# Two transformer blocks on one core: norm factors from sums formed during the output projection, and the next layer's first projection in pairs of tiles

## What is computed

```python
def rms_norm_2(x, g):
    return x * lax.rsqrt(jnp.mean(x * x, axis=-1, keepdims=True) + EPS) * g

def mixer_layer(x, ctx, ...):
    hx = rms_norm_2(x, g_pre) * (1.0 + scale_x) + shift_x
    hc = rms_norm_2(ctx, g_pre) * (1.0 + scale_c) + shift_c
    ... = in_proj(hx, w_in), in_proj(hc, w_in)      # first of it: the latent q (384 columns)
    ...                                             # three branches, attention
    out_x = merge_branches(...) @ w_o
    x = x + gate_x * rms_norm_2(out_x, g_post)
    if update_ctx:                                  # only in the first of the two layers
        ctx = ctx + gate_c * rms_norm_2(out_c, g_post)
```

## Time and profile before

| | us |
|---|---|
| median of three runs (lowest, highest) | 2761.8 (2761.8, 2762.77) |
| the profiled execution | 2760.01 |
| its span in the trace | 2758.2 |
| PE busy in it | 2548.8 (92%) |
| DVE / ACT / POOL busy | 1156.1 / 874.9 / 532.6 |

### The profile page before, as it was taken

How to read it: one execution, slowest core, us unless ns; L and a number is a source line. 1 busy time by engine, 2 the same in 40 slices (tenths; PEclk the granted TensorE clock), 3 DMA queues, 4 the chain that set the end, 5 groups by cost and what they waited for, 6 DMA issues and landing times.

```text
span 2758.2 us, 33891 instructions
## 1 busy us (share of the span) xinstructions
PE 2548.8 (92%) x13851; PEld 1979.4 (72%) x13851; DVE 1156.1 (42%) x1907; ACT 874.9 (32%) x1589; POOL 532.6 (19%) x398
## 2 busy tenths in 40 slices
PE   7888889899999898999989999999698999899998
PEld 5655667677788675578866888888465577678876
DVE  3645544553444426442266223223435533642433
ACT  3325542432222214432145211212324432532222
POOL 3004212321111212220022110122313210221023
PEclk8997999999999899999999999999789999999998
DMA  4231151344422210102200122122110123013232
GB/s 157 78 93 31 47 168 61 108 153 153 153 92 91 87 30 20 39 24 62 84 9 16 46 84 62 46 77 100 48 30 21 39 69 107 1 47 114 77 92 92
DMA packets 188636, 200.59 MB, mean 73 GB/s; under 512 B 15640, under 2 KB 183288, under 8 KB 187970
## 3 DMA queue, kind: packets, MB, share of 16 engines
q1 hardware_dynamic: 184866, 178.23, 21.0%
q10 hardware_dynamic: 3616, 20.19, 1.9%
HBM read 187.92 MB, written 10.49 MB: 72 GB/s over the span
## 4 chain that ended last, share of the span: by engine, by line
PE 82%; DVE 7%; ACT 5%; POOL 3%; issue 3%; DMA 1%; ACTq 0%; POOLq 0%; SPq 0%; DVEq 0%
PE PS L682 20%; PE PS L683 20%; PE PS L685 20%; PE PS L764 5%; PE PS L791 4%; PE PS L777 2%; PE PS L1110 2%; DVE ST L1778 1%; ACT SA L1266 1%; PE PS L726 1%; DVE WL L1710 1%; POOL RB L2412 1%; PE PS L833 1%; PE PS L889 1%; PE PS L860 1%
## 5 line engine op out<-in xcount | busy, mean ns | idle before, releaser
L682 PE MATMUL PS<-HH,WH 128*128 128x512 f32 x2144 | 797.0, 372 | 36.7 <-POOL HL L2417 19.6
L683 PE MATMUL PS<-HL,WH 128*128 128x512 f32 x2144 | 764.6, 369 | 0.0
L685 PE MATMUL PS<-HH,WL 128*128 128x512 f32 x2144 | 692.4, 367 | 0.0
L1710 DVE TENSOR_TENSOR WL<-WB,WH 128x2048 fp32r<-128x2048 f32 (+2 forms) x150 | 313.2, 2088 | 640.6 <-ACT WH L1199 632.7
L682 PEld LDWEIGHTS PS<-HH,WH 128*128 128x128 f32 x2144 | 405.4, 189 | 155.4 <-issue 29.7
L683 PEld LDWEIGHTS PS<-HL,WH 128*128 128x128 f32 x2144 | 405.9, 189 | 73.9 <-issue 1.9
L685 PEld LDWEIGHTS PS<-HH,WL 128*128 128x128 f32 x2144 | 366.7, 189 | 46.6
L1199 ACT ACTIVATE WH<-WB 128x2048 fp32r<-128x2048 f32 (+2 forms) x150 | 256.3, 1708 | 362.3 <-PE PS L685 290.5
L2437 POOL TENSOR_SCALAR SA<-SA,ST 128x768 f32<-128x768 f32 (+3 forms) x80 | 141.1, 1764 | 451.8 <-DVE ST L1792 451.8
L2412 POOL TENSOR_TENSOR RB<-RB,SA 128x512 f32<-128x512 f32 (+2 forms) x68 | 92.7, 1363 | 429.6 <-ACT SA L1216 428.0
L1266 ACT ACTIVATE SA<-PS,ST 128x768 f32<-128x768 f32 (+3 forms) x160 | 118.8, 743 | 94.7 <-DVE ST L1778 94.3
(11 more groups left out here) (324 smaller groups left out, 3420.5 us busy)
## 6 DMA issues: line engine op xcount, KB each, us to landing
WB<-in_w_in_dram SPq DMA_DIRECT2D x67, 1024.0 KB, 5.3
WB<-in_w_ff_dram SPq DMA_DIRECT2D x32, 1024.0 KB, 5.5
WB<-in_w_mod_dram SPq DMA_DIRECT2D x24, 1024.0 KB, 5.3
WB<-in_w_branch_dram SPq DMA_DIRECT2D x24, 512.0 KB, 3.5
WB<-in_w_o_dram SPq DMA_DIRECT2D x8, 1024.0 KB, 5.6
XTc<-xd ACTq DMA_DIRECT2D x2, 3072.0 KB, 10.1
WB<-in_cmp_w_dram SPq DMA_DIRECT2D x4, 1024.0 KB, 5.5
WB<-in_w_mkv_dram SPq DMA_DIRECT2D x4, 1024.0 KB, 5.2
```

Of the source, the lines that this page charges most:

```text
L682: pe.matmul(D[0:m, d + o:d + o + w], h, xh[:, o:o + w], start=first, stop=False)
L683: pe.matmul(D[0:m, d + o:d + o + w], h, xl[:, o:o + w], start=False, stop=False)
L685: t = pe.matmul(D[0:m, d + o:d + o + w], lo, xh[:, o:o + w], start=False, stop=last)
L1710: dve.tensor_tensor(WL[s % NH][:, 0:b.kt, 0:b.cols], WB[b.n % NW][:, 0:b.kt, 0:b.cols], WH[s % NH][:, 0:b.kt, 0:b.cols].bitcast(F32), ALU. ...
```

## The change

It has four parts.

1. **o0 and the two norms.** ACT alone empties the PSUM tiles of `o0`: it squares straight from PSUM (scale 0.5), copies to `OT` already multiplied by gate and gain (`GM`, to which the 0.5 has moved), and for layer 0 also squares that copy ("oo") and the residual's tiles ("xx"). DVE forms the products of residual and `OT` ("cross") and their sum in `AC1`, and the sum of "xx" in `AC0`; POOL adds "oo" in `AC2` beside the squares of `o0`. The next norm's sum is then xx + 2·r·cross + r²·oo, with r the first norm's factor. PE sums seven sets of columns, DVE combines them on 6 columns (`uv`), ACT roots, and both factors are spread. The wide sums, the wide root and the wide inverse go.
2. **The loop over layer 1's tiles.** Scaling `OT` (DVE, now without the gain), the residual addition (POOL) and the tiles' norm go through one loop, tile by tile. In both layers the shift of even tiles moves from DVE to ACT (in place, then the copy to `HH`). The spill goes in four DMAs, the last after tile 7. The weights of `ql`'s second block are split inside the loop.
3. **`ql` in a pair.** `linear_pair` computes output tiles 0 and 1 together: per input tile both tiles' matmuls. Layer 0's ctx factor is made ahead of the x factor.
4. **Sums without the last addition, tables ahead.** For `h0x` and `o1`, PE sums the accumulated seven squares and the eighth apart (`sum_columns_late`), so POOL's last addition goes. Activations of one column (`TL`) load ACT's table for Exp before the attention and for Sqrt before `o{l}`.

```diff
+            def linear_pair(name, x, n, freed, ready):
+                b = of[name][0]
+                Ds = [slot((name, j), *freed(j)) for j in range(2)]
+                wh, wl = whole(b)
+                for k in range(b.kt):
+                    for r in ready(k):
+                        pe.wait_ge(*at(*r))
...
+                    for j, D in enumerate(Ds):
...
+            def sum_columns_late(N, nf, n, *freed):
+                D = slot(("norm", N), *freed)
+                pe.wait_ge(*at("nadd", N, nf - 2))
+                add_columns(D, 0, n, RB[rb[N]], True, False)
+                pe.wait_ge(*at("sq", N, nf - 1))
+                add_columns(D, 0, n, SA[sa[N, nf - 1]], False, True).then_inc(*done("nsum", N))
...
+                    D = slot(("norm", N), ("on", l, 7))
+                    pe.wait_ge(*at("nadd", N, 6))
+                    add_columns(D, 0, nt, RB[rb[N]], True, False)
+                    E = slot(("norm", "h1"), ("hn", "h1x", 7), ("hn", "h1c", 7))
+                    pe.wait_ge(*at("xadd", 7))
+                    add_columns(E, 0, nt, AC[0], True, False)
+                    pe.wait_ge(*at("nadd", "oo", 6))
+                    add_columns(E, 6, nt, AC[2], False, False)
+                    pe.wait_ge(*at("sq", N, 7))
+                    add_columns(D, 0, nt, SA[sa[N, 7]], False, True).then_inc(*done("nsum", N))
+                    pe.wait_ge(*at("cross", 6, "sum"))
...
+                    spread_columns(N, nt)
+                    spread_columns("h1", nt)
```

ACT, layer 1's loop and the end of the layer:

```diff
+                        shift = MOD[:, l, f, s_:s_ + 1]
+                        if f % 2 == 0:
+                            act.wait_ge(*at("hm", N, f))
+                            D = SD[sd["hn", N, f]][:, 0:n]
+                            act.activation(D, D, ACT.Identity, bias=shift).then_inc(*done("hb", N, f))
+                            act.wait_ge(*at("hb", N, f))
+                            act.activation(HH[:, f, o:o + n], D, ACT.Copy).then_inc(*done("hh", N, f))
...
+                    if l == 1 and f % 2:
+                        act.wait_ge(*at("xt_p", 0, f))
+                        act.dma_start(XD[:, f - 1:f + 1, :], XTc[:, f - 1:f + 1, :]).then_inc(...)
                 act.wait_ge(*at("spill", l + 1))
...
+                act.activation(TL[:, :], EP[:, :], ACT.Sqrt)
...
+                    act.activation(D[:, 0:nt], P(N, j)[:, 0:nt], ACT.Square, scale=0.5).then_inc(*done("sq", N, j))
+                    for o, n, s_ in segs[l]:
+                        t = act.activation(OT[:, j, o:o + n], P(N, j)[:, o:o + n], ACT.Copy, scale=GM[:, l, 1, j, s_:s_ + 1])
```

DVE and POOL:

```diff
+                        for f in {3: (0, 1), 4: (2, 3), 5: (4,), 6: (5, 6), 7: (7,)}.get(j, ()):
+                            cross(f)
+                        for f in {3: (1,), 4: (2, 3), 5: (4, 5), 6: (6, 7)}.get(j, ()):
+                            residual(f)
...
+                    dve.wait_ge(*at("nbc", "o0"))
+                    out_part(0)
+                    inverse("h1", 6)
+                    out_part(1)
+                    dve.wait_ge(*at("nbc", "h1"))
                 for f in range(8):
+                    if l and 0 < f < 7:
+                        out_part(f + 1)
+                    if f == 3:
+                        begin(f"ql{l}")
+                    dve.wait_ge(*at(*(("xt_p", 0, f) if l else ("xf", 3, 7))))
...
+                for f in range(8):
+                    if l == 1:
+                        residual(0, f, NT)
+                    if f % 2 == 0:
                         for N, o, n in ((f"h{l}x", 0, NX), (f"h{l}c", NX, NC)):
                             low_half(N, f, HL[:, f, o:o + n], HH[:, f, o:o + n])
```

More of the change, by code:

```diff
@@ L422, in build @@
             ot = sb("ot", 128, 4, 1024, scope=s2)
+            AC, QS = [sb(f"AC{i}", 128, NT, scope=s2) for i in range(3)], sb("QS", 128, 8, scope=s2)
         rows, _ = vec_layout()
@@ L688, in linear @@
                             after(j)
+            def linear_pair(name, x, n, freed, ready):
[5 more added lines that the diff above has]
+                        pe.wait_ge(*at(*r))
+                    xh, xl = x(k)
+                    for j, D in enumerate(Ds):
+                        h, lo = (w[:, k, 128 * j:128 * j + 128] for w in (wh, wl))
+                        for o, w in cols_of(n):
+                            pe.matmul(D[:, o:o + w], h, xh[:, o:o + w], start=k == 0, stop=False)
+                            pe.matmul(D[:, o:o + w], h, xl[:, o:o + w], start=False, stop=False)
+                        for o, w in cols_of(n):
+                            t = pe.matmul(D[:, o:o + w], lo, xh[:, o:o + w], start=False, stop=k == b.kt - 1)
+                        if k == b.kt - 1:
+                            t.then_inc(*done("lin", name, j))
             def linear_tok(b, x, ready, ntok, *freed, pace=0):
@@ L720, in sum_columns, with add_columns @@
                 t.then_inc(*done("nsum", N))
+            def add_columns(D, c0, n, src, first, last):
+                for c in range(n // 128):
+                    t = pe.matmul(D[:, c0 + c:c0 + c + 1], src[:, c * 128:(c + 1) * 128], cm("ones")[:, 0:1],
+                                  start=first and c == 0, stop=last,
+                                  skip_group_check=True)
+                return t
+            def sum_columns_late(N, nf, n, *freed):
[4 more added lines that the diff above has]
+                add_columns(D, 0, n, SA[sa[N, nf - 1]], False, True).then_inc(*done("nsum", N))
             def spread_columns(N, n):
@@ L1162, in tensor_program @@
                 merge(2)
[L1164 removed]
+                drain(linear(f"o{l}", hx(nt), nt, lambda j: [("ot_a", l, j)],
                              lambda k: [("ml_d" if k % 2 else "ml_p", l, k)]))
[L1166 to L1172 removed]
+                N = f"o{l}"
+                if l == 1:
+                    sum_columns_late(N, 8, nt, ("on", l, 7))
+                    spread_columns(N, nt)
+                else:
+                    D = slot(("norm", N), ("on", l, 7))
[9 more added lines that the diff above has]
+                    pe.wait_ge(*at("cross", 6, "sum"))
+                    add_columns(E, 12, nt, AC[1], False, False)
+                    pe.wait_ge(*at("cross", 7))
+                    add_columns(E, 12, nt, SD[sd["cross", 7]], False, True)
+                    pe.wait_ge(*at("sq", "oo", 7))
+                    add_columns(E, 6, nt, SA[sa["oo", 7]], False, True).then_inc(*done("nsum", "h1"))
+                    spread_columns(N, nt)
+                    spread_columns("h1", nt)
             for h in range(2):
@@ L1212, in sq @@
                     D = taken(rb, RB, N, freed)
+                elif f == last:
+                    D = taken(sa, SA, (N, f), freed)
                 else:
-                    D = taken(sa, SA, (N, f), ("nadd" if freed is not None else "nacc", N, f))
+                    D = taken(sa, SA, (N, f), ("nadd", N, f))
                 act.wait_ge(*at(*ready))
@@ L1598, in scalar_program @@
                 root(f"kvn{l}", NT, 256)
+                act.activation(TL[:, :], EP[:, :], ACT.Exp)
                 for half in range(2):
@@ L2380, in vector_program, with cross, residual @@
                 m_low(7)
+                N = f"o{l}"
+                def cross(f):
+                    D = AC[1] if f == 0 else taken(("cross", f), ("nsum", "h1") if f == 7 else ("cross", f, "sum"))
+                    dve.wait_ge(*at("ot_a", l, f))
+                    dve.tensor_tensor(D[:, 0:nt], XTc[:, f, 0:nt], OT[:, f, 0:nt], ALU.mult).then_inc(*done("cross", f))
+                    if 0 < f < 7:
+                        dve.wait_ge(*at("cross", f))
+                        dve.tensor_tensor(AC[1][:, 0:nt], AC[1][:, 0:nt], D[:, 0:nt], ALU.add).then_inc(*done("cross", f, "sum"))
+                def residual(f):
+                    dve.wait_ge(*at("sq", "xx", f))
+                    if f > 1:
+                        dve.wait_ge(*at("xadd", f - 1))
+                    dve.tensor_tensor(AC[0][:, 0:nt], AC[0][:, 0:nt], SA[sa["xx", f]][:, 0:nt], ALU.add).then_inc(*done("xadd", f))
                 for j in range(8):
```

168 lines of the change are left out of this document (87 added, 81 removed).

## The result

The changed kernel takes 2735.1 us as the median of four runs (2733.8 to 2738.4), beside 2762.3 for the kernel before on the same chip (2761.8 to 2762.8): the ratio is 0.9899, 95% interval 0.9885 to 0.9912. It is 27.2 us faster. Forecast were 2750 and a range of 2740 to 2758: the sign was right, the size less than half of what came.

A forecast was written before the change was run, and what follows sets the result against it. TensorE was taken as the bound nearly everywhere, so only stretches where it waits could pay. Terms 7.8 - 2 + 3.6 + 2.5 = 11.9 us off 2760.0 gave 2748.1, as a median 2750, range 2740 to 2758.

The forecast's parts named there:

- B: Between the layers, o0's end to kvl1: DVE starts 11.2 us earlier, but longer loop rounds leave kvl1 2 us later.
- D: Table loads: Exp's 1.28 us load before each layer's first attention unit moves to where ACT idles, 2.5 us less.
- A: Layer 0's entry: computing the first two ql output tiles as a pair ends 7.8 us earlier; bounds 9.5 and 0.
- worst case: Whole kernel, without the slow-DVE rival: the terms' low ends, 5 - 6 + 2.8 + 2, gain only 3.8 us, 2758.
- C: End of the kernel: POOL's last addition and the table load go, 3.6 us less (2.8 to 4.2).
- the page's sum: Table loads at 1.38 us more draining each, by the skill page: C and D some 4 us better, time 2746.
- The Sqrt load ... nothing: In front of o0 and o1: the load delays a weight split needed 8 us later, so costs nothing.
- 1, the loop overlaps: Layer 1's tile loop: POOL never kept waiting, so 14 us gained instead of 2 lost, 2734; chance 12%.
- 2, DVE late beside o0: Beside o0: 21 DVE operations at 2.2 us each end late and delay TensorE's sums, 6 us slower, 2768; chance 6%.
- 3, the clock stays low in the pair: Layer 0's ql pair: TensorE's clock stays low, so A gains nothing, 2758; chance 12%.
- 4, all sums at the full clock: Sums between the layers: all passes run at full clock, so B gains 5 us instead, 2743; chance 12%.

The follow-up runs named there:

- the base: The changed kernel run once more with nothing edited, as reference for the follow-ups: 2734.1 us, ratio 0.9904 to the kernel before.
- TL alone: The kernel before with the four-byte-wide tile TL only allocated, no instruction added, moving everything allocated behind it by 32 bytes: 2757.8 us, ratio 0.9988.
- early-factor order: Changed kernel, but o0's norm factor summed and spread first, so DVE's scalings and POOL's additions run beside the remaining sums: 2717.4 us, ratio 0.9838.

## Why the forecast was right and wrong, point by point

The result lies below the range. Three things failed: the balance at the end of B, the size of D, and a term for the addresses that the sum did not have.

**A, right.** 8.5 us where 7.8 stood: DVE's start stayed (7.4 us behind the feed-forward stage against 7.7), the pair ran without a gap. With single tiles 6.9 of it went, so most of A is the pair. The forecast had nothing for what follows: the sums over `ql` and `kvl` ran in part at the low level in every trace with layer 0's pair (0.72 over them in the base, 1.00 in the kernel before), and 1.3 to 3.4 us went back. They did so too without a pair in the traces with TL alone (65.2), with Sqrt's load besides (65.3) and with the pad ahead of `HH` on the kernel before (65.7); so the pair is not needed for it. What sets where the clock falls was not tested. The forecast's worst case counts A at 5 us, though its own bound for A was 0; the result lies at the other end.

**B, the chain right, the balance wrong.** Sums to 15.9 us behind `o0` (forecast 15.8), DVE's start 22.9 (23.1), rounds of 9.1 to 10.1 us (9.4), POOL idle 3.6 us in each (3 to 4). The step that failed is the chain of spill and weights to "`kvl1`", at "2022.3. **2 us more** than before". The spill's last quarter was issued 58.3 us behind `o0` (forecast 61.1) and done 3.3 us after that, not 4.3; the weights' low half was ready (2006.6) before the third tile's matmuls were through. So `kvl1` started right behind them, 68.6 us behind `o0`, where the forecast had 71.9 and the kernel before 69.9. With 1.3 gained instead of 2 lost the term is off by 3.3. The second traces give 2.2 up to `kvl1`'s copy.

**C, right.** 4.3 on average where 3.6 stood (2.8 to 4.2), 3.5 between the first two traces; the sums took 1.9 us where 2.1 stood. From the last sum to the scaling the forecast's times left 2.2 us, and it took 2.6 to 2.7 in both kernels, without the load.

**D, mis-sized.** "2.5 us less" was the load's own length, twice. In its place it measured 5.1, and the run without it lost 8.6. The missing part in its place is the granted clock, which had fallen behind the wait in these traces; in the one with TL alone it had not in layer 0, and there the load cost its length only. The forecast had cited the Trainium skill ("ScalarE: Activation LUTs", What ACT_TABLE_LOAD costs), which puts 1.38 us of draining on each load. The trace has the activation 0.02 us behind the load, and TensorE's wait grew by 1.28 us, so no such drain shows. By the page's sum the forecast would have been nearer, for another reason. "The Sqrt load ... nothing" was true of the delay that it meant: no matmul of `o0` waited. But the load left a chain between the layers too, worth 2.3 by one pair of traces, which the forecast had inside B without a price.

**A term was missing.** Nothing in the forecast concerned the allocation of TL. It is 3 to 6 us, visible only as 395 against 391 ns in matmuls that the change does not touch.

**The rivals.** *1, the loop overlaps*: not in this kernel. Its counter-argument, that the low half stands in POOL's queue behind the addition, was the right one, and changing just that order gave 8 us. *2, DVE late beside o0*: the 21 operations took 0.94 to 2.6 us, 1.42 on average (forecast 1.3, harmless up to 1.4), and let TensorE wait only 0.38 us. *3, the clock stays low in the pair*: no, 0.88 over it. *4, all sums at the full clock*: no, the first 12 passes took 1.40 us, the next 24 took 4.11, then it was 2.70 for 12. In the early-factor order the passes took 0.12 to 0.13 us each until 11 us behind o0's end, and only the last set 2.70 for 12; there TensorE has the spread's 128-column matmuls between them.

Of the 15 us between forecast and result, an estimate from these differences gives 3 to 6 to addresses, 3 to 6 to D and 3 to 4 to B, less 2 to 3 given back behind A. What remains is within the spread between executions: the kernel before ran from 2756.8 to 2767.1 over all its runs.

## What to carry to other kernels

Price a stall on a chain by its length and by what TensorE's matmuls behind it take at the level to which the clock has fallen; here 1.28 us cost 1.3 where the clock stayed high and 2.5 to 4.1 where it fell. Where two norms follow each other, finish what depends on the first factor while the second one's sums are still being made, and never put an operation directly behind one on which it depends through other engines if an independent one is at hand. Before believing a difference of a fifth of a per cent, compare runs that were made beside each other, compare the durations of untouched instructions, and see whether an allocation moved; where TensorE is the bound, try the addresses of data against weights.

## What the runs showed of the hardware

- A 512-column matmul on split fp32 (low half of the data, high weights) took 391 ns or 395 ns by whether data and weights both start at odd or both at even multiples of 32 bytes, or one at each. Over this kernel that is 14 to 19 us for `HH` and `HL` (2717.4 against 2703.5 and 2698.5, in three groups of runs), with one or two 32-byte pads as the whole edit. The Trainium skill ("SBUF — State Buffer", SBUF: two separate sides) has it that on the engines' side only the port pair that VectorE and GpSimd share causes contention, and that TensorE never waits on anyone. Whether the 4 ns are a wait, and for what, no run here shows; why parity matters was not tested.
- A table load of 1.28 us in front of an activation delayed TensorE by 1.28 us (2.12 us idle instead of 0.84), and the eight matmuls behind took 2.85 us at the full clock in one trace and 4.29 in another, in which it had fallen.
- The first 930 us of unchanged instructions took 926.8 to 935.1 us in traces of kernels with the same addresses there, and 930.1 and 935.1 in two traces of one program; the differences lie in stretches in which the granted clock is at the low level in one trace and at the high one in the other.
